# Four token-quarter sums move from VectorE's program to GpSimd's, with finer waits before the products

## The reference

```
h = rms_norm(x);  u = h @ W_in          # inputs of four mixers
mixers: neighbourhood attention (na), mLSTM (ml), convolution (cv), grouped attention (at)
g = sigmoid(h @ W_gate + b)             # 4 x 1024 gate columns
x += (sum_b g_b * P_b(mixer_b)) @ W_out
x += hierarchical_moe(rms_norm(x))      # top group, top 2 experts of it
```

## Time and profile before

| what | value |
|---|---|
| median of three runs | 2245.08 us |
| profiled execution, its own time | 2239.99 us |
| span of it | 2238.2 us |
| PE busy | 2045.4 us (91%) |
| DVE busy | 965.6 us (43%) |
| ACT busy | 524.9 us (23%) |
| POOL busy | 339.3 us (15%) |

### The profile page before, as it was taken

One profiled execution on the slowest core, in us unless ns is written; L12 is line 12 of the kernel. 1 busy time (PEld: TensorE's weight loads), 2 busy tenths in 40 slices (PEclk: granted clock), 3 DMA queues, 4 the chain that ended last, 5 costly groups with the idle time before them and its releaser, 6 DMA issues. The chain is left out here.

```text
span 2238.2 us, 24086 instructions
## 1 busy us (share of the span) xinstructions
PE 2045.4 (91%) x8840; PEld 1274.6 (57%) x8840; DVE 965.6 (43%) x1820; ACT 524.9 (23%) x1114; POOL 339.3 (15%) x276
## 2 busy tenths in 40 slices
PE   7799999999999997999498999999999999969990
PEld 3455556555655554888245555645555655558870
DVE  1677615343545644111256773243444475431114
ACT  2133312344330001111122332124353100101111
POOL 1322220111110011000223122102211100110003
PEclk9999999999999998999799999999999999979995
DMA  5355557111116622998441121212110274159955
GB/s 203 151 198 210 232 196 299 54 66 66 66 57 249 239 92 106 368 365 308 177 182 38 66 80 52 76 38 97 73 66 26 108 284 195 57 230 343 371 203 178
DMA packets 67188, 361.85 MB, mean 162 GB/s; under 512 B 5760, under 2 KB 6144, under 8 KB 54016
## 3 DMA queue, kind: packets, MB, share of 16 engines
q1 hardware_dynamic: 42160, 276.40, 32.8%
q10 hardware_dynamic: 18000, 58.73, 6.5%
q0 software_dynamic: 6912, 25.17, 3.1%
HBM read 249.13 MB, written 111.15 MB: 161 GB/s over the span
## 5 line engine op out<-in xcount | busy, mean ns | idle before, releaser
L674 PE MATMUL bank<-x,ring 128*128 128x384 f32 x1056 | 374.6, 504 | 27.1 <-issue 27.1
L674 PE MATMUL bank<-hT,ring 128*128 128x384 f32 x1056 | 360.2, 490 | 3.2 <-issue 3.2
L674 PEld LDWEIGHTS bank<-x,ring 128*128 128x128 f32 x1056 | 199.7, 195 | 187.5 <-issue 73.8
L674 PEld LDWEIGHTS bank<-hT,ring 128*128 128x128 f32 x1056 | 195.9, 190 | 144.9 <-issue 21.4
L832 ACT ACTIVATE sums<-bank 128x384 f32<-128x384 f32 x132 | 64.9, 491 | 306.1 <-PE bank L674 304.4
L994 DVE SCALAR_TENSOR_TENSOR reg_a<-cvx,pp,reg_a 128x783 f32<-128x783 f32 x120 | 130.3, 1086 | 4.3
L659 PE MATMUL bank<-ring,hT 128*128 128x256 f32 (+1 forms) x384 | 125.4, 486 | 0.0
L972 DVE SCALAR_TENSOR_TENSOR gbuf<-bank,sums 128x384 f32<-128x384 f32 x96 | 53.5, 558 | 155.3 <-PE bank L674 108.4
L1719 DVE SCALAR_TENSOR_TENSOR prob<-prob,bank 128x256 f32<-128x256 f32 x30 | 12.6, 421 | 229.4 <-ACT prob L1539 229.4
L659 PEld LDWEIGHTS bank<-ring,hT 128*128 128x128 f32 x384 | 72.5, 190 | 49.1 <-issue 43.7
L506 PE MATMUL bank<-ring,hT 128*128 128x512 f32 x192 | 88.2, 614 | 5.3 <-ACT hT L525 5.3
(11 more groups left out here) (258 smaller groups left out, 2991.1 us busy)
## 6 DMA issues: line engine op xcount, KB each, us to landing
ring<-in_wd SPq DMA_DIRECT2D x29, 2048.0 KB, 9.8
blocks<-hT SPq DMA_DIRECT2D x16, 3072.0 KB, 21.3
gate_dram<-gbuf ACTq DMA_DIRECT2D x64, 384.0 KB, 2.3
ring<-gate_dram SPq DMA_DIRECT2D x16, 1536.0 KB, 6.4
oT<-in_we SPq DMA_DIRECT2D x8, 2048.0 KB, 11.4
ring<-in_we SPq DMA_DIRECT2D x8, 2048.0 KB, 11.9
wide<-in_we SPq DMA_DIRECT2D x8, 2048.0 KB, 11.1
reg_b<-in_we SPq DMA_DIRECT2D x8, 2048.0 KB, 11.4
```

The lines of the kernel that those rows point to most:

```text
L674: mm = nc.tensor.matmul(bank[i % 2][:, 0:HALF], w[:, k, :], a[:, k, :], start=(k == 0 and r in (0, 1, 3)), stop=(k == 3), skip_group_check ...
```

## The change

The four sums leave VectorE's program, and with them VectorE's waits for `ht_ev` (all of hT evicted) and `x_saved`. GpSimd's program gets them: s_0 and s_1, then the power of rope part 0, then s_2 and s_3. TensorE waits for s_1 (which implies s_0) ahead of products 2 and 3, for s_2 ahead of product 4 and for s_3 ahead of product 5, where it waited for all four ahead of product 2.

```
@@ TensorE, product
-                if r == 2:
-                    pe.wait_ge(s_done, 4)
+                if 2 <= r < 6:
+                    pe.wait_ge(s_done, {2: 2, 3: 2, 4: 3, 5: 4}[r])
@@ VectorE, mix_vector
-            if layer:
-                dve.wait_ge(x_saved, 16 * T)
-            else:
+            if layer == 0:
                 dve.wait_ge(consts_done, 16)
-            dve.wait_ge(ht_ev, 2 * T)
-            done(tt(s_of[0], quarter[1][0], quarter[1][1], ALU.add), s_done)
-            done(tt(s_of[1], s_of[0], quarter[0][0], ALU.subtract), s_done)
-            done(tt(s_of[2], quarter[0][0], quarter[1][0], ALU.subtract), s_done)
-            done(tt(s_of[3], quarter[0][1], s_of[1], ALU.subtract), s_done)
@@ GpSimd, mix_gpsimd
+            def token_sums(n):
+                for m in n:
+                    a, b, op = ((quarter[1][0], quarter[1][1], ALU.add), (s_of[0], quarter[0][0], ALU.subtract),
+                                (quarter[0][0], quarter[1][0], ALU.subtract), (quarter[0][1], s_of[1], ALU.subtract))[m]
+                    done(tensor_(s_of[m], a, b, op), s_done)
@@ GpSimd, the loop over the steps
-                if kind == "rope" and key[1] == 0:
-                    power(1 + key[0], 18 * key[0], 18)
+                if kind == "rope" and key == (0, 0):
+                    if layer:
+                        pool.wait_ge(x_saved, 16 * T)
+                    else:
+                        pool.wait_ge(h_done, T)
+                        pool.wait_ge(h_sq, T)
+                    pool.wait_ge(ht_ev, 2 * T)
+                    token_sums(range(2))
+                    power(1, 0, 18)
+                    token_sums(range(2, 4))
+                elif kind == "rope" and key == (1, 0):
+                    power(2, 18, 18)
```

## The result

The changed kernel is a little slower: 2248.69 us, the median of 20 runs, against 2244.01 us for the kernel before in 20 runs. The ratio is 1.0024, with a 95% interval of 1.0015 to 1.0033, which is 3.4 to 7.4 us. The forecast was +6.7 us.

The account below looks back on a forecast made before the run. PE, busy 91%, was bound where product 3 waits 9.7 us a layer for VectorE's late eviction. Line 972 would start 3.33 us later per layer, 6.7 in all: 2245.08 + 6.7 = 2251.8 us, range 2247.5 to 2256.0.

Parts of the forecast that it names:

- The power ends 3.1 us earlier, no more: GpSimd, layer 0: rope part 0's power, behind s_0 and s_1, ends at 67.83 instead of 70.95 us.
- gain of 10.1 us: VectorE, per layer: 7.17 us of sums plus about 3 us of earlier rope work, if the power came at once.
- s_2 is ahead of line 1001, and the engines take turns: Rope part 0: GpSimd's s_2, s_3 and two VectorE instructions alternate, each waiting out the other's; 6.4 us a layer.
- Rival 2: No turn-taking between s_2, s_3 and rope's pieces: 3.1 us a layer faster, 2238.8 us; chance 0.08.
- The size of a sum: GpSimd: a sum of 1536 elements takes 3.5 us, scaled from rows of 512 elements at 1.27 us.
- Rival 1: GpSimd's long sums take 3.81 us each: 4.6 us a layer, +9.1 in all, 2254.2 us; chance 0.15.
- The finer waits give nothing: TensorE's separate waits for the sums bring no gain: product 2 passes without idle, s_2 and s_3 precede product 3.
- The clock: TensorE at product 3: the longer hole costs no new fall, 0 us, up to 1.5 a layer if recovery is later.
- rival 4: TensorE's clock comes back later after the hole: 1 to 1.5 us a layer more, 2254 us; chance 0.07.
- The total: Whole kernel: 2 x 3.33 = 6.7 us slower, median 2251.8 us; chance 0.60.
- rival 3: PE's later waits on line 674 take up at best half the delay: about 2248 us; chance 0.10.
- same: Verdict of no change, within 0.2% (4.5 us): a median of 2240.6 to 2249.6 us; chance 0.13.

Follow-up runs that it names:

- two sums left out: Changed kernel without s_2 and s_3, products 4 and 5 multiplying what x holds there; 2270.54 us, total not to be compared because the routing differed.
- One wait: Changed kernel with TensorE waiting once for all four sums ahead of product 2, as before the change; 2249.08 us, 1.0026 to the kernel before.
- square first: Kernel before, sums still on VectorE, only piece 0 of rope part 0 moved ahead of VectorE's wait for hT; 2232.97 us, 0.9935.
- rope first: Kernel before, sums still on VectorE, all three pieces of rope part 0 ahead of the hT wait, TensorE's waits as in the changed kernel; 2226.86 us, 0.9917.
- power first: Changed kernel with GpSimd making rope part 0's power ahead of its wait for hT and all four sums; 2230.56 us, 0.9933 to the kernel before.
- two sums on each engine: Changed kernel with s_2 and s_3 back on VectorE, behind its eviction of product 1; 2239.82 us, 0.9982 to the kernel before.

## Why the prediction was right

The sign and the mechanism were right, step by step, and the time within its range:

- *The power ends 3.1 us earlier, no more.* It ended at 67.94, against 70.95 before; by the sum it was 67.83. (hT was ready 0.3 us later in this execution, so the step itself is worth 3.3 us.) The gain of 10.1 us that leaving VectorE seems to promise was never to be had, because the power waited for hT behind two sums of 3.42 us.
- *s_2 is ahead of line 1001, and the engines take turns.* It was: s_2 at 67.92, line 1001 at 68.05. The waits cost 8.97 - 2 x 1.36 = 6.3 us, 6.4 forecast. Rival 2, no turn-taking, fell with rows of 4.51 and 4.46 us, and "two sums left out" puts a hole of 6.49 us where it had 6.6.
- *The size of a sum.* This term was off by a little: 3.5 us forecast, 3.42 measured. With four sums on the path that is 0.3 us a layer, and so the hole grew by 3.03 us and not 3.33. Rival 1 (3.81) fell.
- *The finer waits give nothing.* "One wait": 1.0026 against 1.0024.
- *The clock.* 0 was put on it. Product 3 took 4.94 and 4.62 us, against 4.53 and 4.52: half a microsecond in all, on the side of rival 4 and far below its price.
- *The total.* Two holes of 3.03 and 0.5 us of clock, less 0.4 us by which PE's next wait was shorter (1.27 against 1.62 and 1.58 against 1.61): 6.2 us can be seen in the place itself. The medians differ by 4.7, with 3.4 to 7.4 as the interval of the ratio, so nothing need have been taken up later. Whether 1 us was (rival 3) the runs can't tell.

The forecast of 2251.8 us was 3.1 us too high. 1.1 of that is the kernel before, whose median is 2244.01 us over 20 runs and was 2245.08 over the three on record, and 2.0 is the difference of the medians, 4.7 for 6.7. As a ratio the forecast was 1.0030, inside the measured interval. The verdict is closer than the chances make it look. The prediction let "slower" begin at 2249.6 us, with 0.79 on it, and gave 0.13 to "same"; 2248.69 lies just on the side of "same". That the kernel is slower is shown by the comparison of 20 runs with 20, whose interval leaves out 1, and not by that line. The lower bound of the range, 2247.5, was said to be half of the delay; half would be 2248.4, and the median lies above that by 0.3 us.

The two profiled executions differ by more, 2250.50 - 2239.99 = 10.5 us. 3.9 us of that lie between the layers: 1.26 in PE's wait for the first norm of layer 1 (25.27 against 24.01) and 2.57 in one block of an expert that ran at the lower clock (9.98 against 7.41). No instruction of the change is there.

What the prediction missed is not in its sum: it never asked what the idle 10.93 us of VectorE were worth if nothing were moved to GpSimd at all. They were worth 15 us ("square first") to 19 us ("rope first"). It did name the other loss, the power behind two sums, and "power first" and the comparison with "square first" bear it out.

## What to carry to other kernels

Before work is moved to an idle engine, ask what that engine's queue already holds that the others wait for, and whether it shares a way to memory with the engine that is to be relieved: two instructions of VectorE and two of GpSimd that both read SBUF ran one after the other, however idle the page showed GpSimd. Look first at the order on the late engine itself. Four sums that were in the way left no hole once rope's work, which was ready, went ahead of a wait of 10.93 us. And place a moved instruction by two things: what the other engine does at that time, and what stands behind it in its new queue. s_0 and s_1 held up nothing while VectorE idled and still cost 3.2 us a layer, since the power stood behind them; s_2 and s_3 cost 6.3 us a layer beside rope's pieces. A gain against the kernel before doesn't say which part of an edit brought it: "two sums on each engine" gains 4 us, and without its two sums on GpSimd it gains 15.

## What the hardware showed beyond the forecast

Even a short hole can cost TensorE's clock. In "square first" PE stood still for 3.26 us, from 72.54 to 75.80, and went on at the higher clock; then, in windows of 1 us (columns as in the earlier trace rows):

```profile
75.00:76.00 1.00, 0.20 (x1) 0.23 (x2) 0.66 (x2) 0.00 (x0) 0.82 (x1) 1.00 1.00 414
76.00:77.00 1.00, 1.00 (x3) 0.45 (x3) 0.00 (x0) 0.00 (x0) 1.00 (x1) 0.53 1.06 438
77.00:78.00 1.00, 1.00 (x3) 0.63 (x2) 0.00 (x0) 0.00 (x0) 1.00 (x1) 0.50 0.98 406
...
79.00:80.00 1.00, 1.00 (x4) 0.55 (x3) 1.00 (x1) 0.00 (x0) 0.92 (x2) 0.76 0.99 410
80.00:81.00 1.00, 1.00 (x6) 0.71 (x5) 0.96 (x2) 0.56 (x2) 1.00 (x1) 1.00 1.04 426
```

The granted clock fell to its lower level, 1.2 GHz, after PE was busy again, and product 3 took 4.51 us, as after the hole of 9.72 us. A hole of 3.3 us and one of 9.7 us paid the same 1.8 us on top, and only "rope first", without a hole, paid nothing. Such a penalty belongs in the sum of an edit that removes a hole, and not in that of one that shortens it from 9.7 to 3.3 us. Over the holes in these traces product 3 took 4.35 to 5.46 us, with no order by the hole's length. Below 3 us it went either way: the wait of 2.24 us ahead of product 6 was followed by a pair of 7.09 us in layer 1 of "two sums on each engine", and by pairs of 5.40 us in both layers of "rope first". What decides between them, these traces don't show.
